# Attention layers of a hybrid encoder: the logits of two heads one behind the other

## The chip, the cores and the metric

The kernel runs on one core of one Trainium2 chip. Its time is the device time of one launch in microseconds (us). Before the change the median of 3 runs is 1270.73 us, from 1269.79 to 1271.33.

## The reference

Four layers over a sequence of 256 tokens of width 1024, all in float32. Layer 0 and layer 3 mix tokens with differential attention, layer 1 with a gated linear recurrence, layer 2 with a gated short convolution; every layer also has a 4-head cross-attention into 256 memory tokens, an output projection, a layer norm, a gated feed-forward part with a convolution of width 3, and a second layer norm. The attention, which the change concerns, is (cut):

```python
# differential attention, 6 heads, each with two maps of 64 columns
q = q.reshape(b, s, DA_HEADS, 2, DA_HD) * (DA_HD ** -0.5)
k = k.reshape(b, s, DA_HEADS, 2, DA_HD)
logits = jnp.einsum('bqhmd,bkhmd->bmhqk', qb, k).astype(jnp.float32) + bias
probs = jax.nn.softmax(logits, axis=-1)
w = (probs[:, 0] - lam * probs[:, 1]).astype(v.dtype)
o = jnp.einsum('bhqk,bkhe->bqhe', w, v)
o = _rms_norm(o, subln) * (1.0 - lam_init)
# cross-attention into the memory, 4 heads of 64 columns
probs = jax.nn.softmax(jnp.einsum('bshd,bmhd->bhsm', q, km), axis=-1)
recalled = jnp.einsum('bhsm,bmhd->bshd', probs, vm)
y = jnp.concatenate([mixed, recalled], axis=-1) @ w_o[layer]
```

## The kernel before

All weights stream from memory once, in chunks of two units of 128x1024 numbers. Each unit goes through three steps: its load into a ring of 5 raw buffers, a rounding to fp32r on ScalarE (`w_hi`, item "hi"), and the residual of that rounding on VectorE (`w_lo`, item "lo"). A matmul with weights is then three passes: high by high, high by low, low by high. A unit is rounded as soon as the half that used its buffer five units ago is done, so it is ready about four halves ahead of its use.

`make_schedule` (from L72) writes one list of items by hand. Every engine walks through the same list and does its own part of each item, in that order, so an item that waits on an engine holds all later items of that engine. A chunk contributes in this order: "hi" and "lo" of unit 2c+4, the first half of its matmuls, the items of the row with an even number, "hi" and "lo" of unit 2c+5, the second half (behind which ScalarE copies the result out of its bank: `post`), the items of the row with an odd number. In an attention layer the chunks behind XQ are QK0 to QK5 (queries and keys of one head), V0 to V2 (values of two heads) and the four chunks WO of the output projection. Chunk number n in this order has the rows 2n and 2n+1: row 13 stands behind V0, row 14 between the halves of V1, row 15 behind V1, row 16 between the halves of V2. In layer 0 two chunks for the memory come in ahead, and the rows are moved by 4.

The items of the attention are:

- "xlog" and "log" (TensorE L814, L825): the logits of two memory heads or of the two maps of one head, four matmuls of 64 rows by 256 columns in float32, which take two passes each. They fill two of the four banks ACC; item number n takes the banks 0 and 1 when n is even, 2 and 3 when it is odd, and waits until logits n-2 have been read. VectorE takes the row maxima (L1335; for "log" together with adding the bias, L1342, into `lg`).
- "xexp" and "exp" (ScalarE L1071): four exponentials with their sums. "xprob" and "prob" (VectorE L1359 to L1374): the probabilities.
- "xturn" and "turnw" (TensorE L837, L846): the transposes of the probabilities, into the side banks, with copies by ScalarE (L1081, L1086).
- "xpv" (L857) and "pv" (L870): probabilities by values. Behind the second head of a pair ScalarE copies the pair's output (L1092) and squares it (L1095).
- "ms" (VectorE L1384), then a power on GpSimd (L1453), and "tok" (VectorE L1390): the RMS norm of a pair. "scale" (TensorE L895, ScalarE L1101, VectorE L1400): its transposes, and the split of the result into `mixT_hi` and `mixT_lo`, the input of the output projection. Transposes of "scale" and of "turnw" use the same side bank, so a "turnw" behind a "scale" waits for that split.
- "seed" (ScalarE L1055): the output projection adds into the four banks ACC, which are first filled with the scaled residual stream, two banks per item. A seed waits until the last logits in its banks have been read, and WO's first matmul waits for all four.

`post` of QK number u waits for the logits of head u-2, because the two buffers of `qk` alternate. The two buffers of `prob` alternate too: a "prob" waits for the transposes of two items before.

Of the kernel before, what the change touches and what calls it, by code (L numbers as in the profile page):

```python
# [60 lines left out]
def layer_kind(layer):  # L61
    return ("attn", "hgrn", "conv")[layer % 3]


def make_schedule():
# [12 lines left out]
    def split_units(u):  # L78
        items.extend([("lo", u)] if u in rounded else [("hi", u), ("lo", u)])
# [32 lines left out]
    for layer in range(DEPTH):  # L112
        kind = layer_kind(layer)
        it = lambda name, *a: (name, layer, *a)
        chunk("F", "XQ", layer, 0)
        if layer == 0:
            items.extend([("bias_rows",), ("turn", "mem", 0)])
        if kind == "attn":
            order = [("F", "QK", h) for h in range(HEADS)] + [("T", "V", p) for p in range(PAIRS)]


            at = {0: [it("xlog", 0)], 1: [it("xexp", 0)], 2: [it("xprob", 0), it("xlog", 1)],
                  3: [it("xexp", 1), it("log", 0)], 4: [it("exp", 0), it("xprob", 1)],
                  5: [it("xturn", 0), it("log", 1)], 6: [it("exp", 1), it("prob", 0)],
                  7: [it("xpv", 0), it("log", 2)], 8: [it("xturn", 1), it("exp", 2), it("prob", 1)],
                  9: [it("xpv", 1), it("turnw", 0), it("log", 3)], 10: [it("exp", 3), it("prob", 2)],
                  11: [it("turnw", 1), it("log", 4)], 12: [it("exp", 4), it("prob", 3)], 13: [it("turnw", 2), it("log", 5)],
                  14: [it("exp", 5), it("prob", 4), it("pv", 0), it("pv", 1)],
                  15: [it("turnw", 3), it("ms", 0), it("tok", 0)], 16: [it("prob", 5), it("scale", 0)],
                  17: [it("turnw", 4), it("pv", 2), it("pv", 3)], 18: [it("turnw", 5), it("ms", 1), it("tok", 1)],  # L130
                  19: [it("scale", 1), it("pv", 4), it("pv", 5)], 20: [it("ms", 2), it("tok", 2)], 22: [it("scale", 2)]}
            at[13].append(("seed", 2 * layer, 0))
            at[15].append(("seed", 2 * layer, 1))
            if layer == 0:

                order[1:1] = [("F", "KM", 0), ("T", "VM", 0)]
                at = {h + 4: row for h, row in at.items()}
                at[0] = [("turn", "mem", 1)]
                at[5].append(("prepare",))
        elif kind == "conv":  # L140
            order = [("F", "CG", 0), ("F", "CG", 1), ("F", "CB", 0), ("F", "CG", 2), ("F", "CG", 3), ("F", "CB", 1),
                     ("F", "CG", 4), ("F", "CG", 5), ("F", "CB", 2)]
            at = {0: [it("xlog", 0), it("xexp", 0), it("xlog", 1), it("xexp", 1)], 1: [it("xprob", 0), it("xprob", 1)],
                  4: [it("xturn", 0)], 5: [it("xpv", 0)], 8: [it("xturn", 1)], 9: [it("xpv", 1)]}
            at.setdefault(9, []).extend([("seed", 2 * layer, 0), ("seed", 2 * layer, 1)])
        else:
            order = []
            for p in range(PAIRS):
                order += [("F", "FF", p), ("F", "FB", p), ("F", "HQ", p)]
            order += [("T", "HV", p) for p in range(PAIRS)]  # L150
            order += [("F", "HG", p) for p in range(PAIRS)]
            at = {0: [it("xlog", 0), it("xexp", 0), it("xlog", 1), it("xexp", 1)], 1: [it("xprob", 0), it("xprob", 1)],
                  4: [it("xturn", 0)], 5: [it("xpv", 0)], 6: [it("xturn", 1)], 7: [it("xpv", 1)]}
            at[26], at[28] = [("seed", 2 * layer, 0)], [("seed", 2 * layer, 1)]

            for p, first in enumerate((7, 14, 21)):
                for n in range(LEVELS + 1):
                    at.setdefault(first + n, []).append(it("level", p, n))
                    if n + 1 < LEVELS:
                        at[first + n].append(it("keys", p, n + 1))  # L160

            for p in range(PAIRS):
                c = len(chunks) + 3 * p
                at.setdefault(6 * p + 2, []).append(("gates", c))
                at.setdefault(6 * p + 4, []).append(("gates", c + 1))
                at.setdefault(6 * p + 5, []).append(it("sums", p))
                at.setdefault(6 * p + 6, []).extend([("q0", c + 2), it("queries", p, 0)])
                at.setdefault(6 * p + 7, []).insert(len(at[6 * p + 7]) if p else 0, it("queries", p, 1))
                at.setdefault(2 * (4 * PAIRS + p) + 2, []).append(("outgate", len(chunks) + 4 * PAIRS + p))
            for h, more in {20: [it("hpv", 0)], 22: [it("ms", 0)], 23: [it("tok", 0)], 24: [it("hpv", 1)],  # L170
                            25: [it("ms", 1)], 26: [it("scale", 0), it("tok", 1)], 29: [it("scale", 1)], 30: [it("hpv", 2)],
                            31: [it("ms", 2)], 32: [it("tok", 2)], 33: [it("scale", 2)]}.items():
                at.setdefault(h, []).extend(more)

        order += [("O", "WO", (n, pair)) for n, pair in enumerate((3, 0, 1))]
        for n, (form, role, index) in enumerate(order):
            chunk(form, role, layer, index, between=at.get(2 * n, []), after=at.get(2 * n + 1, []),
                  held=role == "WO" and index[0] == 2)

        def close(form, role, index, following):  # L180

            nonlocal norms
            c, m = len(chunks), norms
            chunks.append((form, role, layer, index))
            last = m == 2 * DEPTH - 1
            items.extend([("half", c, 0), ("stats", m, 0), ("hi", 2 * c - 1 + AHEAD), ("half", c, 1)])
            items.extend([("norm", m, 0), ("lo", 2 * c - 1 + AHEAD), ("hi", 2 * c + AHEAD)])
            items.append(("stats", m, 1))

            items.extend([("norm", m, 1), ("turn", m, 0)] if following else [("norm", m, 1)] if last else  # L190
                         [("turn", m, 0), ("norm", m, 1)])
            if following:
                items.append(("lo", 2 * c + AHEAD))
                chunks.append(following)
                items.extend([("half", c + 1, 0), ("part", c + 1)])
            elif not last:

                items.append(("warm",))
                items.append(("early", c + 1))
            items.append(("hi", 2 * c + 1 + AHEAD))  # L200
            if not last:
                items.append(("turn", m, 1))
            if following:
                items.append(("half", c + 1, 1))
            else:
                items.append(("lo", 2 * c + AHEAD))
            items.append(("lo", 2 * c + 1 + AHEAD))
            if following:
                split_units(2 * c + 2 + AHEAD)
                split_units(2 * c + 3 + AHEAD)  # L210
            norms += 1

        more = layer + 1 < DEPTH
        close("O", "WO", (3, 2), ("F", "KM", layer + 1, 0) if more else None)

        for g in range(GROUPS):
            chunk("F", "UA", layer, g)
            chunk("F", "UB", layer, g, after=[("seed", 2 * layer + 1, t) for t in range(TT)] if g == 0 else ())
            if 1 <= g <= GROUPS - 3:
                chunk("O", "DN", layer, (g - 1, g - 1))  # L220
        for g in (GROUPS - 3, GROUPS - 2):
            chunk("O", "DN", layer, (g, g), held=g == GROUPS - 2)
        close("O", "DN", (GROUPS - 1, GROUPS - 1), ("T", "VM", layer + 1, 0) if more else None)
# [4 lines left out]
def trunk_kernel(nc, stream, x, mem, rel_bias, ln, lam, subln, lower, hnorm, cconv, fconv,  # L228
                 ident_c, onehot_c, masks_c, out):
    chunks, items = make_schedule()  # L230
    nchunks = len(chunks)
    n_last_o = {layer: None for layer in range(DEPTH)}
# [1300 lines left out]
```

## Time and profile before

| what | value |
|---|---|
| median of 3 runs | 1270.73 us (1269.79 to 1271.33) |
| the profiled execution, its own time | 1269.29 us |
| its span, from the first to the last instruction | 1267.5 us |
| TensorE busy | 1252.7 us |
| VectorE busy | 1016.2 us |
| ScalarE busy | 728.8 us |
| mean granted clock of TensorE | 0.999 of full speed |

The profile comes from one execution. Its views name an engine as PE (TensorE), PEld (its weight loads, which overlap PE), DVE (VectorE), ACT (ScalarE), POOL (GpSimd); L12 is line 12 of the kernel. The chain of waits follows the work that ended last back from step to step; in it a matmul stands with the time that it adds, since matmuls overlap in a pipeline. In the timeline a row gives the start, the time from the first start to the last end of a run of like instructions, and the idle time in front. The end of a matmul is modelled, so distances between starts are what counts on TensorE. Layer 0's attention lies at about 33 to 125 us, layer 3's at about 973 to 1064 us.

### The profile page before, as it was taken

Reading aid. Unit: us, or ns where it says so; the run is one execution under the profiler, and the core shown is the slowest. Engines: PE = TensorE matmul, PEld = TensorE weight load, DVE = VectorE, ACT = ScalarE, POOL = GpSimd, SP = SyncE. Lnnn points to the kernel's source line nnn. Section 1 sums busy time; section 2 is a strip of 40 time slices with the busy share of each in tenths; the row PEclk is TensorE's granted clock in tenths of the full one; section 3 lists DMA queues with packets and bytes.
Section 4 is the critical chain, followed back from the end, with each engine's and each line's share of the span. In section 5 each row is a group of like instructions: output and inputs, shape, how many; then the busy total and the mean of one; then the engine's idle time right before and its main releaser. Section 6 shows DMA issues by size and latency. Waiting matters only on the chain.

```text
span 1267.5 us, 20453 instructions
## 1 busy us (share of the span) xinstructions
PE 1252.7 (99%) x7778; PEld 1108.1 (87%) x7778; DVE 1016.2 (80%) x1576; ACT 728.8 (58%) x1184; POOL 20.8 (2%) x29
## 2 busy tenths in 40 slices
PE   8999999999999999999999999999999999999997
PEld 6988888888999988888889998888889898888886
DVE  5775898888869888988888768988888776888887
ACT  5665665555676554655564635655564774655552
POOL 0000000000000010000000000000000000000000
PEclk9999999999999999999999999999999999999999
DMA  8734465665544345655555664665655443565561
GB/s 294 246 126 138 155 227 188 199 196 173 180 167 133 117 135 170 226 189 194 186 186 177 211 199 172 221 198 186 192 189 172 162 134 116 184 232 195 187 193 58
DMA packets 63389, 228.27 MB, mean 180 GB/s; under 512 B 7446, under 2 KB 9110, under 8 KB 62268
## 3 DMA queue, kind: packets, MB, share of 16 engines
q1 hardware_dynamic: 63292, 226.97, 54.3%
q8 instruction: 62, 1.02, 0.3%
q14 instruction: 35, 0.29, 0.1%
HBM read 225.88 MB, written 1.06 MB: 179 GB/s over the span
## 4 chain that ended last, share of the span: by engine, by line
PE 92%; DVE 5%; DMA 1%; issue 1%; ACT 1%; SPq 0%; DVEq 0%
PE pair L686 26%; PE acc L749 20%; PE pair L689 13%; PE pair L700 6%; PE pair L701 5%; PE pair L702 5%; PE pair L712 2%; PE pair L714 2%; PE pair L716 2%; PE pair L914 2%; PE acc L728 1%; PE acc L730 1%; PE acc L729 1%; DMA raw<-in_stream 1%; DVE w_lo L1132 1%; PE acc L825 1%
## 5 line engine op out<-in xcount | busy, mean ns | idle before, releaser
L1132 DVE TENSOR_TENSOR w_lo<-raw,w_hi 128x1024 fp32r<-128x1024 f32 x404 | 487.7, 1222 | 114.4 <-ACT w_hi L932 113.7
L932 ACT ACTIVATE w_hi<-raw 128x1024 fp32r<-128x1024 f32 x404 | 424.4, 1057 | 222.7 <-PE pair L689 69.1
L686 PE MATMUL pair<-xT,w_hi 128*128 128x512 f32 x1392 | 437.1, 395 | 1.0 <-DVE xT L1296 1.0
L689 PEld LDWEIGHTS pair<-xT,w_lo 128*128 128x128 f32 x1392 | 261.5, 188 | 61.5
L689 PE MATMUL pair<-xT,w_lo 128*128 128x256 f32 x1392 | 273.5, 278 | 0.0
L686 PEld LDWEIGHTS pair<-xT,w_hi 128*128 128x128 f32 x1392 | 214.3, 189 | 4.0 <-issue 1.5
L700 PE MATMUL pair<-xT,w_hi 128*128 128x256 f32 x592 | 171.3, 289 | 0.6 <-DVE xT L1296 0.6
L701 PE MATMUL pair<-xT,w_hi 128*128 128x256 f32 x592 | 167.4, 283 | 0.0
L702 PE MATMUL pair<-xT,w_lo 128*128 128x256 f32 x592 | 167.3, 283 | 0.0
L963 ACT ACTIVATE hid<-pair 128x512 f32<-128x512 f32 x88 | 52.4, 596 | 129.4 <-PE pair L689 128.6
L700 PEld LDWEIGHTS pair<-xT,w_hi 128*128 128x128 f32 x592 | 113.3, 191 | 6.9 <-issue 5.1
L701 PEld LDWEIGHTS pair<-xT,w_hi 128*128 128x128 f32 x592 | 113.5, 192 | 0.0
L702 PEld LDWEIGHTS pair<-xT,w_lo 128*128 128x128 f32 x592 | 113.4, 192 | 0.0
L1164 DVE TENSOR_TENSOR hid<-pair,hid 128x512 f32<-128x512 f32 x88 | 60.7, 690 | 50.9 <-ACT hid L963 50.9
L749 PE MATMUL acc<-w_hi,gT_hi 128*128 128x512 f32 x304 | 93.9, 390 | 0.0
L749 PE MATMUL acc<-w_lo,gT_hi 128*128 128x512 f32 x304 | 93.6, 389 | 0.0
L749 PE MATMUL acc<-w_hi,gT_lo 128*128 128x512 f32 x304 | 93.6, 389 | 0.0
L1009 ACT ACTIVATE cv<-hid,fconv_w 128x256 f32<-128x256 f32 x176 | 79.3, 499 | 16.0 <-DVE hid L1164 15.6
L1149 DVE SCALAR_TENSOR_TENSOR cv<-hid,fconv_w,cv 128x255 f32<-128x255 f32 x176 | 77.4, 481 | 3.1
L1145 DVE SCALAR_TENSOR_TENSOR cv<-hid,fconv_w,cv 128x255 f32<-128x255 f32 x176 | 76.9, 479 | 0.0
L749 PEld LDWEIGHTS acc<-w_lo,gT_hi 128*128 128x128 f32 x304 | 57.1, 188 | 12.2
L749 PEld LDWEIGHTS acc<-w_hi,gT_lo 128*128 128x128 f32 x304 | 57.1, 188 | 11.9
(185 smaller groups left out, 1605.5 us busy)
## 6 DMA issues: line engine op xcount, KB each, us to landing
raw<-in_stream SPq DMA_DIRECT2D x404, 512.0 KB, 4.5
gains<-in_ln SPq DMA_DIRECT2D x8, 1024.0 KB, 8.7
bias<-bias_scratch SPq DMA_DIRECT2D x2, 1152.0 KB, 8.8
x_tok<-in_x SPq DMA_DIRECT2D x2, 512.0 KB, 5.2
y_tok<-in_mem SPq DMA_DIRECT2D x1, 1024.0 KB, 11.7
out<-x_tok SPq DMA_DIRECT2D x4, 256.0 KB, 2.0
masks_in<-in_masks_c SPq DMA_DIRECT2D x1, 512.0 KB, 7.8
fconv_w<-in_fconv SPq DMA_DIRECT2D x1, 264.0 KB, 7.6
```

The source lines that it names most:

```text
L686: pe.matmul(bank, w_hi[:, slot, kk * P:(kk + 1) * P], xT[:, kk].rearrange("p a s -> p (a s)"), start=(kk == 0), stop=(kk == KT - 1), skip_ ...
L689: last = pe.matmul(bank[:, 0:SEQ], w_lo[:, slot, kk * P:(kk + 1) * P], xT[:, kk, 0, :], start=False, stop=(kk == KT - 1), skip_group_check ...
L700: pe.matmul(bank, w_hi[:, slot, at], a_hi(k, every), start=(k == 0), stop=False)
L701: pe.matmul(bank, w_hi[:, slot, at], a_lo(k, every), start=False, stop=False)
L702: last = pe.matmul(bank, w_lo[:, slot, at], a_hi(k, every), start=False, stop=(k == KT - 1))
L749: last = pe.matmul(ACC[2 * t + h][:], b(i, tok), w[:, slot, h * 512:h * 512 + 512], start=False, stop=False, skip_group_check=True)
L932: nc.scalar.activation(w_hi[:, u % SPLIT, :], raw[:, u % RAW, :], ACT.Copy).then_inc(hi_ready, 1)
L1009: last = nc.scalar.activation(cv[:, w, i, :], hid[:, w, i, :], ACT.Copy, scale=fconv_w[:, layer, 1, first + i:first + i + 1])
L1132: v.tensor_tensor(w_lo[:, u % SPLIT, :], raw[:, u % RAW, :], w_hi[:, u % SPLIT, :].bitcast(F32), ALU.subtract).then_inc(lo_ready, 1)
L1145: last = v.scalar_tensor_tensor(dst[i][:, 1:SEQ], src[i][:, 0:SEQ - 1], weights(0, i), dst[i][:, 1:SEQ], ALU.mult, ALU.add)
L1149: last = v.scalar_tensor_tensor(dst[i][:, 0:SEQ - 1], src[i][:, 1:SEQ], weights(2, i), dst[i][:, 0:SEQ - 1], ALU.mult, ALU.add)
L1164: v.tensor_tensor(hid[:, w], PAIR[proj_ord[c] % 2][:, :, 0:SEQ], hid[:, w], ALU.add).then_inc(hid_ready, 1)
```

## The change

The schedule of the attention layers is rewritten; no instruction is added or removed. The two "xlog" stand in one row, and the six "log" in three rows as pairs, (0, 1), (2, 3) and (4, 5), one behind the other, so that they take all four banks. "xturn" (0) comes behind the first pair, "xpv" (0) and (1) and "xturn" (1) get rows of their own, exps and probs move by one to three rows, and the seeds of the sums stand one row later each, at the end of their rows.

```diff
-            at = {0: [it("xlog", 0)], 1: [it("xexp", 0)], 2: [it("xprob", 0), it("xlog", 1)],
-                  3: [it("xexp", 1), it("log", 0)], 4: [it("exp", 0), it("xprob", 1)],
-                  5: [it("xturn", 0), it("log", 1)], 6: [it("exp", 1), it("prob", 0)],
-                  7: [it("xpv", 0), it("log", 2)], 8: [it("xturn", 1), it("exp", 2), it("prob", 1)],
-                  9: [it("xpv", 1), it("turnw", 0), it("log", 3)], 10: [it("exp", 3), it("prob", 2)],
-                  11: [it("turnw", 1), it("log", 4)], 12: [it("exp", 4), it("prob", 3)], 13: [it("turnw", 2), it("log", 5)],
-                  14: [it("exp", 5), it("prob", 4), it("pv", 0), it("pv", 1)],
-                  15: [it("turnw", 3), it("ms", 0), it("tok", 0)], 16: [it("prob", 5), it("scale", 0)],
+            at = {0: [it("xlog", 0), it("xlog", 1)], 1: [it("xexp", 0)], 2: [it("xexp", 1), it("xprob", 0)],
+                  3: [it("xprob", 1)], 5: [it("log", 0), it("log", 1), it("xturn", 0)],
+                  6: [it("exp", 0), it("xpv", 0)], 7: [it("exp", 1), it("prob", 0), it("xturn", 1)],
+                  8: [it("prob", 1), it("xpv", 1)], 9: [it("turnw", 0), it("log", 2), it("log", 3)],
+                  10: [it("exp", 2)], 11: [it("turnw", 1), it("exp", 3), it("prob", 2)],
+                  12: [it("prob", 3)], 13: [it("turnw", 2), it("log", 4), it("log", 5)],
+                  14: [it("exp", 4), it("pv", 0), it("pv", 1)],
+                  15: [it("turnw", 3), it("exp", 5), it("prob", 4), it("ms", 0), it("tok", 0)], 16: [it("prob", 5), it("scale", 0)],
                   17: [it("turnw", 4), it("pv", 2), it("pv", 3)], 18: [it("turnw", 5), it("ms", 1), it("tok", 1)],
                   19: [it("scale", 1), it("pv", 4), it("pv", 5)], 20: [it("ms", 2), it("tok", 2)], 22: [it("scale", 2)]}
-            at[13].append(("seed", 2 * layer, 0))
-            at[15].append(("seed", 2 * layer, 1))
+            at[14].append(("seed", 2 * layer, 0))
+            at[16].append(("seed", 2 * layer, 1))
```

## Rows read from the trace of the kernel before

**Rows 1.** The page, part 1: busy us, share of the span and instructions.
```profile
PE 1252.7 (99%) x7778; PEld 1108.1 (87%) x7778; DVE 1016.2 (80%) x1576; ACT 728.8 (58%) x1184; POOL 20.8 (2%) x29
```
**Rows 2.** Waits of TensorE over the whole span: total us, times, longest.
```profile
PE pair L846 <- DVE mixT_lo L1400: 0.7, 2, 0.3
```
**Rows 3.** Chain of waits, start us and us: logits in layers 3 and 1.
```profile
976.71 1.07 PE acc L814 x8
977.78 0.32 PE pair L700
...
340.01 2.03 PE acc L814 x16
```
**Rows 4.** Chain of waits, layer 3: xturn, xpv, turnw behind xpv, turnw alone.
```profile
994.89 0.87 PE pair L837 x8
...
1002.79 1.02 PE pair L857 x8
...
1012.71 0.59 PE pair L846 x4
...
1020.32 0.44 PE pair L846 x4
```
**Rows 5.** Timeline of TensorE, layer 3: start us, us, instruction, idle before it.
```profile
1032.20 1.95 PE L870 MATMUL pair<-v_tok,probT 128*128 128x128 f32 x16
...
1040.17 0.60 PE L895 MATMUL pair<-ident,a_out 128*128 128x128 f32 x4
...
1043.36 0.28 PE L716 MATMUL pair<-w_hi,xT 128*128 128x256 f32 x1
1043.98 0.63 PE L846 MATMUL pair<-ident,prob 128*128 128x128 f32 x4 [0.34 <-DVE mixT_lo L1400]
```
**Rows 6.** Timeline of ScalarE, layer 3: outputs' copy, rounding, seed 1, rounding.
```profile
1034.18 0.60 ACT L1092 ACTIVATE a_out<-pair 128x512 f32<-128x512 f32 x1 [1.06 <-PE pair L870]
...
1035.67 1.08 ACT L932 ACTIVATE w_hi<-raw 128x1024 fp32r<-128x1024 f32 x1
...
1038.03 1.12 ACT L1055 ACTIVATE acc<-x_tok 128x512 f32<-128x512 f32 x2
1039.07 1.06 ACT L932 ACTIVATE w_hi<-raw 128x1024 fp32r<-128x1024 f32 x1
```
**Rows 7.** Timeline of VectorE, layer 3: residual, ms, tok, prob's first instruction, split.
```profile
1036.79 1.22 DVE L1132 TENSOR_TENSOR w_lo<-raw,w_hi 128x1024 fp32r<-128x1024 f32 x1 [2.85 <-ACT w_hi L932]
1037.93 0.16 DVE L1384 TENSOR_SCALAR ms_eps<-ms_sum 128x4 f32<-128x4 f32 x1
1039.22 0.69 DVE L1390 TENSOR_TENSOR a_out<-a_out,ms_r 128x512 f32<-128x512 f32 x1 [1.13 <-POOL ms_r L1453]
...
1041.30 0.17 DVE L1365 RECIPROCAL row_inv<-row_sum 128x4 f32<-128x4 f32 x1
...
1043.09 0.74 DVE L1400 SCALAR_TENSOR_TENSOR mixT_lo<-pair,sub_gain,mixT_hi 128x512 fp32r<-128x512 f32 x1
```
**Rows 8.** Timeline of ScalarE, layer 3: post, rounding, transposed copies, first exp, rounding.
```profile
1002.82 0.38 ACT L953 ACTIVATE qk<-pair 128x256 f32<-128x256 f32 x1 [1.13 <-PE pair L702]
...
1003.37 1.06 ACT L932 ACTIVATE w_hi<-raw 128x1024 fp32r<-128x1024 f32 x1
1008.42 1.09 ACT L1081 ACTIVATE xprobT<-pair 128x512 f32<-128x512 f32 x2 [4.00 <-PE pair L837]
1009.39 0.51 ACT L1071 ACTIVATE ex<-lg,neg_max 128x256 f32<-128x256 f32 x1
...
1011.37 1.05 ACT L932 ACTIVATE w_hi<-raw 128x1024 fp32r<-128x1024 f32 x1
```
**Rows 9.** Timeline of TensorE, layer 3: xturn(1) and, one half later, xpv(1).
```profile
1007.79 1.04 PE L837 MATMUL pair<-ident,prob 128*128 128x128 f32 x8
...
1011.62 1.09 PE L857 MATMUL pair<-xprobT,vm 128*64 128x256 f32 x8
```
**Rows 10.** Stretch 18 to 22 us: length, busy us of each engine, granted clock, DMA.
```profile
18.00:22.00 4.00, 2.33 (x15) 1.29 (x14) 1.23 (x1) 2.12 (x4) 0.00 (x0) 1.00 0.67 262
```

## The prediction

> **What bounds the kernel now.** First the engines' shares of the span: TensorE is busy 1252.7 of 1267.5 us, VectorE 1016.2, ScalarE 728.8 [rows 1]. So a us that TensorE no longer spends is a us of the span, and work of the other engines counts only where TensorE comes to a wait and finds it unfinished. Then TensorE's waits over the whole run: the one in the attention layers that the change touches is the memory transposes of head 4 (L846) waiting for the split of the first normed pair (L1400), 2 times, 0.7 us in all, once in layer 0 and once in layer 3 [rows 2]. Both layers show the same instants 939.2 us apart, so I work in layer 3 and double.
>
> **What the joins are worth.** In the chain of waits a weight matmul takes 0.12 us after another weight matmul. The logits of one head (8 passes) take 1.07, and the weight matmul behind them 0.32, 0.20 more than usual: 1.27 for logits that stand alone [rows 3]. Layer 1 already puts two logits one behind the other: 2.03 for 16 passes [rows 3], with the same 0.20 behind them 2.23; two alone cost 2.54. The other small groups: transposes of a memory pair (xturn) 0.87 with nothing behind them, even in front of logits; memory values (xpv) 1.02, with 0.20 behind when a weight matmul follows; transposes of a head (turnw) 0.44 alone and 0.59 behind xpv [rows 4].
> Before, in program order: xlog0 1.27, xlog1 1.27, log0 1.27, xturn0+log1 0.87+1.07+0.20 = 2.14, xpv0+log2 1.02+1.07+0.20 = 2.29, xturn1 0.87, xpv1+turnw0+log3 1.02+0.59+1.07+0.20 = 2.88, turnw1+log4 0.44+1.07+0.20 = 1.71, turnw2+log5 1.71. Sum 15.41.
> After: the xlog pair 2.23; log0+log1+xturn0, where no row shows transposes behind logits: 2.03 + 0.87, and 0.15 as turnw costs more behind xpv (0.59 against 0.44; bounds 0 and the 0.20 of a weight matmul), 3.05; xpv0 1.22; xturn1 0.87; xpv1 1.22; turnw0+pair 0.44+2.03+0.20 = 2.67; turnw1 0.44; turnw2+pair 2.67. Sum 14.37. That is 1.04 us less in each attention layer (0.99 to 1.19 by the bounds). Three pairs of one kind come together, and xpv loses its neighbour twice, which is why it isn't four times 0.31. Two heads of the mixer in a pair read different buffers than layer 1's pair; if that cost the join all its gain, the term would be 0.
>
> **What the moves cost: the first normed pair.** This is the large term. From the start of pv(0), pv(1) on TensorE (1032.20) to the transposes of the normed pair (scale 0, 1040.17) TensorE has 7.97 us of work of its own [rows 5]: both pv, V1's second half, turnw3, V2's first half. Beside it runs the chain that scale 0 waits for: the copy of the heads' outputs starts 1.98 after pv's start, copy and squares take 1.49, then ScalarE rounds a weight unit, and VectorE's residual of that unit starts 1.12 after the rounding [rows 6, 7]; the residual holds 1.14, ms starts, tok 1.29 later, and tok holds 0.69 and is seen 0.15 after its end (as L846 starts 0.15 after L1400's end, 1043.98 against 1043.83) [rows 5, 7]. Sum 1.98+1.49+1.12+1.14+1.29+0.69+0.15 = 7.86. The slack is 0.11 us.
> The change puts two things in that chain. Seed 0 moves from row 13 to the end of row 14, behind pv(1)'s copy on ScalarE and ahead of the rounding: two copies, 1.04 us until the rounding starts [rows 6]. And prob(4) moves from row 14, where it ran while VectorE had nothing to do, to row 15 ahead of ms(0): the reciprocal to the next instruction is 1.79 [rows 7]. VectorE takes its instructions in order, so ms(0), the power on GpSimd, tok(0) and scale 0 wait for prob(4). exp(4) is no hindrance: counted from turnw2's start, VectorE has log(4)'s maxima at about 4.0 (log(4) is done at 1.6, and prob(3) with a residual holds VectorE to 2.4, then 1.6 for the maxima), four exps of 1.98 end at 6.0, and the copy behind them can't start before 0.52 + 2.03 + 2.98 + 1.98 = 7.5. New chain 7.86+1.04+1.79 = 10.69, TensorE's own work unchanged at 7.97: scale 0 waits 2.72 us, and V2's second half and all behind it with it. Bounds: 0.93 if prob(4) were hidden, 1.68 if the seed were, and 3.2 with one more ScalarE copy of 0.5 in the chain, above the value taken.
>
> **The other waits.** At turnw4 TensorE now waits: the last weight matmul starts at 1043.36, the transposes could follow at 1043.48 and start at 1043.98, 0.50 [rows 5]. After, counted from scale 0's start, TensorE needs 0.35+2.96 = 3.31 (the 3.31 from 1040.17 to 1043.48); VectorE is done with tok 0.23 before scale 0, and takes residual 1.14, prob(5) 1.79, then the split, which turnw4 sees 0.89 after its start: 3.59. Wait 0.28, so 0.22 is won back. exp(5) (row 15) stands behind the copies of V1 and turnw3 and ends about 14.0 us after turnw2's start; prob(5) begins at 16.2 - 0.23 + 1.14 = 17.1: hidden by the wait above. Seed 1 (row 16, 1.04) is over some 3 us before WO's first matmul needs the four sums.
> Early in the layer one transfer gets short. xturn(1)'s copies stand on ScalarE behind exp(1): from the end of QK3's second half 0.19 to see it, 0.55 for post's two copies, four exps 1.98, two transposed copies 1.09, 0.15 to be seen, 3.96 [rows 8]; TensorE goes from xturn to xpv over one half, as here from 1007.79 to 1011.62, in 3.83 [rows 9]. 0.12 us of wait at xpv(1), bounds 0 and 0.4. ScalarE's copy of QK2 now waits for log(0), one group longer; TensorE needs that bank only a chunk later. VectorE takes two heads' maxima in a row (2 times 1.6); w_lo is made four halves (some 12 us) ahead, which covers them, and what is left of the cover is over 8 us. The loads of raw follow the residuals; none moves by more than 3.5 us against the 15 of its ring.
>
> **Sum.** Per layer -1.04 + 2.72 - 0.22 + 0.12 = +1.58; two layers +3.16. The profiled execution took 1269.29 (span 1267.5) and would take 1272.45; against the median 1270.73, which is 1.44 above it, 1273.9.
>
> **A rule against the reading of the joins.** In rows 3 the 16 passes of two heads follow at the pitch of 8, with no overlap, though the halves of a head use different 64 partitions. The Trainium skill, TensorEngine Tiling (Array Packing), Key Properties, says that different tiles can load and multiply in parallel. By that rule the second half of one head could run beside the first half of the next: up to 4 passes of 0.12 in each of the four pairs, 1.9 us per layer more; the trace of layer 1's pair speaks against it.
>
> **Rivals.**
> (a) The wait at scale 0 doesn't come, as the normed pair turns out not to be what its transposes wait for in this order, and only the joins are left: with xpv(1)'s 0.12, 1270.73 - 2 x 0.92 = 1268.9, not slower. For it: TensorE shows no wait there now. Against: the chain's slack is 0.11 and ScalarE and VectorE keep their order. The change is faster as long as less than 0.92 of the 2.72 arrives. 12 in 100.
> (b) The seed is hidden, as ScalarE has room ahead of the rounding elsewhere; prob(4) alone counts: 3.16 - 2.08 = +1.08, 1271.8. Against it: the seed waits behind the copy in program order. 11 in 100.
> (c) The pairs of the mixer's heads gain nothing (other buffers): +2.08 on top, 1276.0. 8 in 100.
> (d) TensorE's clock falls to 1.2 GHz in the new wait of 2.72 us. Around the longest wait of today, 1.67 us between 18 and 22 us, the granted clock stays at 1.00, 2.4 GHz [rows 10]. If V2's second half then ran at double its 2.96: +5.9, 1279.8. 4 in 100. The Trainium skill, TensorE: Matmul & The Clock Gate, section Why this matters for your kernels, warns that idle gaps between bursts of matmuls bring the clock down; no row here shows such a fall.
> (e) Tiles of two heads run side by side, by the rule above: -3.8 on top, 1270.1. 3 in 100.
>
> **Chances and range.** The forecast has 62 in 100, with its own range 1272.7 to 1275.3 (joins and waits each off by some tenths, medians by half a us). A comparison of this kernel tells about 0.2% (2.5 us) from no change. Slower by more: 0.52 of the forecast's 0.62, (c) and (d): 0.64. Within: the rest of the forecast, (b), (e), most of (a): 0.30. Faster: the lower edge of (a): 0.06. The range goes from just below (a)'s value to just short of (c)'s: 1268.5 to 1275.5.
>
> **What would show it.** A new TensorE wait at L895 for a_out of L1390, 2 times, some 2.7 us each; VectorE's order residual, prob, ms, tok with no idle time between the first three; the L814 and L825 passes at 2.03 us for 16; 0.3 us left of the wait at L846; a short wait at L857. Wrong it is if L895 starts on time, if the pairs take 2.14 for 16 passes, or if TensorE waits for w_lo.

## The result, and the profile after

| kernel | median us | lowest to highest | ratio to before, 95% interval |
|---|---|---|---|
| before | 1270.78 | 1269.79 to 1271.33 | |
| changed | 1275.18 | 1272.98 to 1276.9 | 1.0035 [1.0024, 1.0045] |

The change makes the kernel 4.4 us slower; 1273.9 was forecast. The profiled execution of the changed kernel took 1276.9 us (span 1275.1), 7.6 more than the profiled one of before, so its trace has to be read with care: it holds more than the medians differ by.

First the engines' busy time and TensorE's waits over the whole span (us in total, times, longest), in answer to [rows 1] and [rows 2]. Lines of the changed kernel stand one number higher than before, L896 for L895 and so on.

```profile
PE 1255.5 (98%) x7778; PEld 1114.3 (87%) x7778; DVE 1015.0 (80%) x1576; ACT 727.6 (57%) x1184; POOL 20.8 (2%) x29
```
```profile
PE pair L896 <- DVE a_out L1391: 4.9, 2, 2.5
```

A new wait heads the list: the transposes of the first normed pair wait for the normed pair, once per attention layer. L847's wait for L1401 is gone from it. The timeline of TensorE in layer 3 (start us, us, instruction, idle before it) answers to [rows 5]:

```profile
1036.11 1.95 PE L871 MATMUL pair<-v_tok,probT 128*128 128x128 f32 x16
...
1043.96 0.28 PE L717 MATMUL pair<-w_hi,xT 128*128 128x256 f32 x1
1046.71 0.97 PE L896 MATMUL pair<-ident,a_out 128*128 128x128 f32 x4 [2.47 <-DVE a_out L1391]
1047.33 0.56 PE L713 MATMUL pair<-w_hi,xT 128*128 128x256 f32 x1
1047.69 0.41 PE L715 MATMUL pair<-w_lo,xT 128*128 128x256 f32 x1
1047.90 0.41 PE L717 MATMUL pair<-w_hi,xT 128*128 128x256 f32 x1
...
1051.60 0.60 PE L847 MATMUL pair<-ident,prob 128*128 128x128 f32 x4
```

From pv to the transposes it is now 10.60 us, where it was 7.97. And behind the wait something else is to be seen: weight matmuls start 0.21 us apart (1047.69, 1047.90) instead of 0.12. The clock says why (stretch, its length, busy us of PE, PEld, DVE, ACT and POOL with instructions, granted clock, DMA share, GB/s):

```profile
1042.50:1046.50 4.00, 1.74 (x15) 1.53 (x13) 2.81 (x9) 3.07 (x10) 1.01 (x1) 1.00 0.42 131
1046.50:1048.50 2.00, 1.79 (x9) 1.79 (x10) 1.97 (x6) 0.79 (x2) 0.00 (x0) 0.60 0.00 0
1048.50:1050.30 1.80, 1.80 (x11) 1.80 (x10) 1.70 (x4) 1.80 (x3) 0.00 (x0) 0.50 0.72 189
1050.30:1052.30 2.00, 2.00 (x19) 2.00 (x19) 1.23 (x1) 0.59 (x3) 0.00 (x0) 1.00 0.24 92
```

TensorE had been busy without a wait until 2.47 us before; at the wait's end its granted clock goes to the lower level, 1.2 GHz, and stays there for some 3.5 us. Between the two transposes, 1046.71 and 1051.60, lie 4.89 us, against 3.31 of work at full speed and 3.81 before, where 0.50 of it was a wait.

The chain that set the time of the transposes, on VectorE, answers to [rows 7]:

```profile
1041.74 1.23 DVE L1133 TENSOR_TENSOR w_lo<-raw,w_hi 128x1024 fp32r<-128x1024 f32 x1 [4.66 <-ACT w_hi L933]
1042.89 0.17 DVE L1366 RECIPROCAL row_inv<-row_sum 128x4 f32<-128x4 f32 x1
...
1044.67 0.16 DVE L1385 TENSOR_SCALAR ms_eps<-ms_sum 128x4 f32<-128x4 f32 x1
1045.96 0.69 DVE L1391 TENSOR_TENSOR a_out<-a_out,ms_r 128x512 f32<-128x512 f32 x1 [1.12 <-POOL ms_r L1454]
```

and on ScalarE, to [rows 6]:

```profile
1038.09 0.60 ACT L1093 ACTIVATE a_out<-pair 128x512 f32<-128x512 f32 x1 [1.60 <-PE pair L871]
...
1039.59 1.15 ACT L1056 ACTIVATE acc<-x_tok 128x512 f32<-128x512 f32 x2
1040.63 1.08 ACT L933 ACTIVATE w_hi<-raw 128x1024 fp32r<-128x1024 f32 x1
```

Copy and squares from 1038.09, then the seed to 1040.63, the rounding, the residual at 1041.74 (VectorE idle for 4.66 us in front of it), prob(4) to 1044.67, and only then ms. (The description above has exps and probs move by one to three rows. In the diff the exps move by one or two, prob(0), (2) and (4) by one, and prob(1), (3) and (5) keep their rows.)

The joins are there too, in the chain of waits (start us, us), with the order of logits and transposes that no row of before had, in answer to [rows 3] and [rows 4]:

```profile
981.58 2.03 PE acc L815 x16
983.61 0.32 PE pair L701
...
998.20 2.03 PE acc L826 x16
1000.23 1.03 PE pair L838 x8
...
1011.96 1.09 PE pair L858 x8
```

**Where 7.6 us of the two profiled executions went.** From the pair of xlog to WO's long run of matmuls behind pv(5) in layer 3 (before 976.71 to 1054.66, after 981.58 to 1062.25) the changed kernel took 80.67 us against 77.95: +2.72. It divides at three instants that both traces show. Up to pv(0) (1032.20 and 1036.11) the changed kernel is 0.96 us shorter: that is what the joins gave, the short wait at xpv(1) taken off. From pv(0) to the pair's transposes it is 2.63 longer, from there to turnw4 (the transposes of head 4, L847) 1.08 longer, and behind them 0.03 shorter. The same stretch of layer 0 has +2.75. The other 2.1 us lie ahead of the first logits of layer 0, where nothing was changed: the first load took 7.95 us instead of 7.42, and the clock was low from about 22.9 to 26.3 us, behind a wait of 1.72 us; the kernel before has that wait as well, 1.67 us, and no fall behind it:

```profile
22.00:24.00 2.00, 2.00 (x15) 2.00 (x14) 0.91 (x2) 1.54 (x3) 0.00 (x0) 0.73 0.43 122
24.00:26.30 2.30, 2.30 (x12) 2.30 (x12) 1.60 (x2) 0.49 (x1) 0.00 (x0) 0.50 0.69 207
```

That fall at the launch is no part of the change. Of the profiled executions of the kernels below, those of seed_out, fill_wait, scale_first, old_prob_late and old_scale_first have it too; those of prob_back, both_out and old_seeds_late don't, and nor does that of before.

### The profile page after: what moved, and what is told of

The parts are those of the page before. It is cut to its first block, busy times and chain, and to the rows that moved or that the text cites. A ratio compares the mean times of both kernels' runs of the same rounds, so it can differ in the third digit from the quotient of the medians.

```text
span 1275.1 us, 20453 instructions
## 1 busy us (share of the span) xinstructions
PE 1255.5 (98%) x7778; PEld 1114.3 (87%) x7778; DVE 1015.0 (80%) x1576; ACT 727.6 (57%) x1184; POOL 20.8 (2%) x29
## 3 DMA queue, kind: packets, MB, share of 16 engines
q8 instruction: 62, 1.02, 0.3%
## 4 chain that ended last, share of the span: by engine, by line
PE 92%; DVE 5%; DMA 1%; issue 1%; ACT 1%; POOL 0%; SPq 0%; DVEq 0%; ACTq 0%
PE pair L687 25%; PE acc L750 20%; PE pair L690 13%; PE pair L701 6%; PE pair L702 5%; PE pair L703 5%; PE pair L713 2%; PE pair L715 2%; PE pair L717 2%; PE pair L915 2%; PE acc L729 1%; PE acc L731 1%; PE acc L730 1%; DMA raw<-in_stream 1%; DVE w_lo L1133 1%; PE acc L826 1%
```

## The experiments

Eight kernels, each compared with runs of the kernel before on the same chip (its medians there 1270.83 and 1270.56). "Distance" is from the start of pv(0) to the start of the first normed pair's transposes in layer 3; its own work there takes TensorE 7.97 us. "Stretch" is from the start of the xlog pair (or the first xlog) to WO's long run in layer 3, against the 77.95 us of before; it leaves the launch out.

| kernel | median us | ratio, 95% interval | distance us | idle at the pair's transposes, at turnw4 (longest) | stretch us |
|---|---|---|---|---|---|
| changed | 1275.18 | 1.0035 [1.0024, 1.0045] | 10.60 | 2.5, none | 80.67, +2.72 |
| prob_back | 1270.96 | 1.0006 [0.9997, 1.0014] | 8.82 | 0.7, 1.0 | 78.55, +0.60 |
| seed_out | 1271.96 | 1.0011 [1.0002, 1.0020] | 9.56 | 1.4, 0.7 | 78.98, +1.03 |
| both_out | 1276.34 | 1.0038 [1.0024, 1.0052] | 7.97 | none, 2.3 | 80.59, +2.64 |
| fill_wait | 1273.65 | 1.0024 [1.0014, 1.0034] | 10.60 | filled, 0.2 | 79.49, +1.54 |
| scale_first | 1266.90 | 0.9976 [0.9967, 0.9985] | 7.97 | none, none | 76.47, -1.48 |
| old_prob_late | 1274.16 | 1.0030 [1.0018, 1.0042] | 9.55 | 1.4, 0.2 | 79.39, +1.44 |
| old_seeds_late | 1272.37 | 1.0014 [1.0005, 1.0022] | 8.82 | 0.7, 0.2 | 78.65, +0.70 |
| old_scale_first | 1270.08 | 0.9992 [0.9983, 1.0001] | 7.98 | none, none | 77.42, -0.53 |

Small differences of medians have to be read beside the stretch, as the fall of the clock at the launch is worth about 1.5 us and comes unequally often. Profiled executions without any fall have a mean granted clock of 0.999, those with the launch's alone 0.997 or 0.998, that of both_out with two falls in the attention 0.996, the changed kernel's with all three 0.995. Of the two sets of before, 5 of 25 and 12 of 27 executions have 0.999 or more, of prob_back 7 of 11, of scale_first 6 of 10, of old_scale_first none of 11. Why they differ so isn't known, and that an execution without a trace can be sorted in this way is inferred, not shown.

**prob_back**: the changed kernel, prob(4) where it was.

```diff
-14: [it("exp", 4), it("pv", 0), it("pv", 1)],
-15: [it("turnw", 3), it("exp", 5), it("prob", 4), it("ms", 0), it("tok", 0)],
+14: [it("exp", 4), it("prob", 4), it("pv", 0), it("pv", 1)],
+15: [it("turnw", 3), it("exp", 5), it("ms", 0), it("tok", 0)],
```

> The changed kernel with prob(4) back in row 14, behind exp(4); seed 0 stays at row 14's end. Theory (the chain in front of the first normed pair's transposes grew by seed 0, 1.04 us, and prob(4), 1.79 us, over a slack of 0.11): the wait at L896 shrinks from 2.7 us from start to start to 0.9, per layer -1.04 + 0.93 - 0.22 + 0.12 = -0.2, so 1270.4 us, and TensorE's clock, which fell behind the wait of 2.5 us, stays at full speed. Rival (the wait comes from exp(5) or from the pairs of logits, and prob(4)'s place is of no account): the wait stays at 2.5 us and the time near 1275.

The distance fell from 10.60 to 8.82, by prob(4)'s 1.79, and the time by 4.2 us to about that of the kernel before, some of it the clock, which stayed up. The wait at the pair's transposes came out as forecast. What did not is the wait at turnw4: from start to start it is 1.20 us (4.51 - 3.31; 0.99 idle) instead of the 0.28 taken; more of it below. So the median, 0.6 us from the forecast, flatters it: the stretch is +0.60 per layer where -0.2 was worked out. The median seems to hide this because more executions of prob_back than of before have no fall at the launch (those at 0.999: median 1270.77 against 1269.51, +1.3 us, about twice 0.60).

**seed_out**: the changed kernel, seed 0 one row later.

```diff
-at[14].append(("seed", 2 * layer, 0))
+at[15].append(("seed", 2 * layer, 0))
```

> The changed kernel with seed 0 moved on to the end of row 15, behind the rounding that VectorE waits for; prob(4) stays ahead of ms(0). Theory: 1.04 us go from the chain, the wait at L896 is 1.7 us from start to start, per layer -1.04 + 1.68 - 0.22 + 0.12 = +0.54, so 1271.9 us, if the clock stays up after a wait of 1.5 us idle (before, 1.67 us idle left it at full speed); 1 to 2.5 us more where it falls. Rival (the seed is hidden): the wait stays at 2.5 us, 1275 us.

Distance 9.56, by the seed's 1.04 less than 10.60, and 1271.96 us. The rival (b) of the prediction, a hidden seed, has fallen. The clock in the half behind the wait of 1.44 us stayed up, and the time fell by 3.2 us, more than the 2.1 us of the seed in two layers. Here too turnw4 waits longer than forecast (0.67 us idle, 0.88 from start to start), and the stretch is +1.03 instead of +0.54; two layers of that would give 1272.9, so that the median is 1271.96, as forecast, has some luck in it.

**both_out**: both edits.

> The changed kernel with both edits: prob(4) back in row 14 and seed 0 at the end of row 15. Theory: the chain has its old 7.86 us against 7.97, no wait at L896; only the joins are left, per layer -1.04 - 0.2 + 0.12, together -2.3 us: 1268.5 us, faster than before. Rival (the pairs of logits themselves cost something elsewhere): 1270.8 or more with no wait at L896.

This forecast failed, by 8 us and in sign. The wait at the pair's transposes is gone as expected, but turnw4 waits 2.31 us, and the clock falls behind that wait. First TensorE's timeline of this kernel, then VectorE's and ScalarE's, then the granted clock:

```profile
1045.56 0.28 PE L717 MATMUL pair<-w_hi,xT 128*128 128x256 f32 x1
1048.15 0.91 PE L847 MATMUL pair<-ident,prob 128*128 128x128 f32 x4 [2.31 <-DVE mixT_lo L1401]
```
```profile
1041.42 0.69 DVE L1391 TENSOR_TENSOR a_out<-a_out,ms_r 128x512 f32<-128x512 f32 x1 [1.12 <-POOL ms_r L1454]
1044.33 1.23 DVE L1133 TENSOR_TENSOR w_lo<-raw,w_hi 128x1024 fp32r<-128x1024 f32 x1 [2.21 <-ACT w_hi L933]
1045.47 0.17 DVE L1366 RECIPROCAL row_inv<-row_sum 128x4 f32<-128x4 f32 x1
...
1047.26 0.74 DVE L1401 SCALAR_TENSOR_TENSOR mixT_lo<-pair,sub_gain,mixT_hi 128x512 fp32r<-128x512 f32 x1
```
```profile
1041.71 0.50 ACT L1072 ACTIVATE ex<-lg,neg_max 128x256 f32<-128x256 f32 x1
...
1042.20 1.11 ACT L1056 ACTIVATE acc<-x_tok 128x512 f32<-128x512 f32 x2
1043.24 1.05 ACT L933 ACTIVATE w_hi<-raw 128x1024 fp32r<-128x1024 f32 x1
```
```profile
1048.10:1050.10 2.00, 1.95 (x10) 1.98 (x11) 1.03 (x1) 0.60 (x1) 0.00 (x0) 0.56 0.18 74
```

The split of the normed pair (L1401), which turnw4 waits for, stands behind prob(5) and a residual, and that residual (idle 2.21) waits for a rounding which ScalarE does only after exp(5) and the seed. The prediction had written exp(5) off as "hidden by the wait above". It was hidden as long as that wait was there. With it gone, three things stand in front of the split: exp(5) in its new place, row 15 for row 14 (1.97 us, 1040.23 to 1042.20), the seed that this run itself put behind it (1.04), and prob(5) (1.79). How much is exp(5)'s is shown in part only. old_seeds_late below has the same order as prob_back from pv(0) on except that exp(5) is in row 14: there the residual starts without idle time and turnw4 comes 3.67 us behind the pair's transposes, in prob_back the residual is 0.74 idle for the rounding behind exp(5) and turnw4 comes 4.51 behind. No run moves exp(5) alone in the changed kernel, and scale_first below leaves it in row 15 and has no wait, with the seed and prob(5) out of the way.

**fill_wait**: the changed kernel, TensorE busy through most of the wait.

```diff
+FILL = 10
 ... (cut)
+                    if p == 0 and layer_kind(layer) == "attn":
+                        n = proj_ord[last_half]
+                        pe.wait_ge(*proj_read(n - 1))
+                        for _ in range(FILL):
+                            pe.matmul(PROJ[(n - 1) % 2], mixT_hi[:, 6, 0:P], mixT_hi[:, 6:8, :].rearrange("p a s -> p (a s)"),
+                                      start=True, stop=True)
                     pe.wait_ge(tok_ready, ordinal[pos] + 1)
```

> The changed kernel as it is, with 10 matmuls of 512 columns (2.2 us, their result is not used) on TensorE in front of the transposes of the first normed pair in both attention layers, in a bank that nobody uses then. They fill the wait and leave the chain alone. Theory (the wait costs 2.7 us, and the fall of the clock behind it another 1.2 to 1.3 us per layer in the executions where it falls): transposes start at the same distance from the pv matmuls, 10.7 us, the granted clock stays at 1.00 behind them, and the time is 1273.5 to 1274, with less scatter than the 1273.0 to 1276.9 of the changed kernel. Rival (the clock's fall is a matter of the launch and not of the wait): the stretch behind the transposes still runs at 0.5 of full speed, 1275 us.

This separates the wait from the clock. The transposes start at the same distance, 10.60. TensorE's timeline and the granted clock behind them in layer 3:

```profile
1042.96 2.46 PE L897 MATMUL pair<-mixT_hi 128*128 128x512 f32 x10
1045.59 0.66 PE L903 MATMUL pair<-ident,a_out 128*128 128x128 f32 x4 [0.18 <-DVE a_out L1398]
1049.27 0.63 PE L848 MATMUL pair<-ident,prob 128*128 128x128 f32 x4 [0.15 <-DVE mixT_lo L1408]
```
```profile
1046.50:1048.50 2.00, 2.00 (x19) 2.00 (x19) 1.93 (x8) 2.00 (x4) 0.00 (x0) 1.00 0.34 86
```

The clock is at 2.4 GHz, and turnw4 follows 3.68 us behind the transposes, against 4.89 in the changed kernel: the fall costs 1.21 us per layer where it comes. (The low clock stretches 3.31 us of work by 1.58, but with the clock up 0.37 of that would be a wait at turnw4.) In layer 0 it is the same: 3.68 against 4.90. The time is 1273.65, within 1272.4 to 1274.6, and the stretch is +1.54 per layer; the prediction, for waits and joins alone, had 1273.9 and +1.58. The rival of this run has fallen: its profiled execution has the fall at the launch and none in the attention layers, so the one behind the wait comes from the wait. The medians say the same more weakly, as the intervals of the two ratios, [1.0014, 1.0034] and [1.0024, 1.0045], overlap.

**old_prob_late** and **old_seeds_late**: one part of the change each, made alone on the kernel before.

```diff
-14: [it("exp", 5), it("prob", 4), it("pv", 0), it("pv", 1)],
-15: [it("turnw", 3), it("ms", 0), it("tok", 0)],
+14: [it("exp", 5), it("pv", 0), it("pv", 1)],
+15: [it("turnw", 3), it("prob", 4), it("ms", 0), it("tok", 0)],
```

> The kernel before with one part of the change: prob(4) from row 14 to row 15, ahead of ms(0). Theory: the chain grows from 7.86 to 9.65 us against TensorE's 7.97: L896 waits 1.7 us from start to start, L847 0.3 instead of 0.5, per layer +1.46, 1273.7 us. Rival (the old order's idle time on VectorE covers it): no wait at L896, 1270.8 us.

```diff
-at[13].append(("seed", 2 * layer, 0))
-at[15].append(("seed", 2 * layer, 1))
+at[14].append(("seed", 2 * layer, 0))
+at[16].append(("seed", 2 * layer, 1))
```

> The kernel before with the other part: seed 0 from row 13 to the end of row 14, seed 1 from row 15 to the end of row 16. Theory: the chain is 8.90 us against 7.97, L896 waits 0.9 us from start to start, L847 0.3, per layer +0.71, 1272.2 us. Rival (ScalarE has room): 1270.8 us.

Both came out within 0.5 us, and in the stretch within 0.02: +1.44 and +0.70 for +1.46 and +0.71. With the old logits in place, each move alone makes the wait: distances 9.55 and 8.82 for 9.65 and 8.90 forecast. So neither needs the pairs of logits.

**old_scale_first**: the kernel before, prob(5) behind scale 0.

```diff
-16: [it("prob", 5), it("scale", 0)],
+16: [it("scale", 0), it("prob", 5)],
```

> The kernel before with prob(5) behind scale 0 in row 16 and nothing else. Theory: the split follows the residual directly, so L847 no longer waits its 0.5 us, 2 times: 1269.8 us. Rival (prob(5) is then late for turnw5, or the split is held by ScalarE's copy): the wait moves and the time is 1270.8 us or more.

L846's wait is gone, and the next "turnw" isn't late. In time the interval holds both no change and the 1 us forecast, so the medians don't decide. The stretch of the one trace has the 0.5 us: 77.42 against 77.95. In every execution of this kernel the clock (0.997 or 0.998) looks as if it had fallen at the launch.

**scale_first**: the changed kernel's pairs with the four items in a better order.

```diff
-14: [it("exp", 4), it("pv", 0), it("pv", 1)],
-15: [it("turnw", 3), it("exp", 5), it("prob", 4), it("ms", 0), it("tok", 0)], 16: [it("prob", 5), it("scale", 0)],
-at[14].append(("seed", 2 * layer, 0))
+14: [it("exp", 4), it("prob", 4), it("pv", 0), it("pv", 1)],
+15: [it("turnw", 3), it("exp", 5), it("ms", 0), it("tok", 0)], 16: [it("scale", 0), it("prob", 5)],
+at[16].append(("seed", 2 * layer, 0))
```

> The changed kernel with prob(4) back in row 14, prob(5) behind scale 0 in row 16, and seed 0 behind both in row 16, ahead of seed 1. Theory (behind the first wait stands a second chain, exp(5) at its new place, a rounding, a residual, prob(5) and only then the split that turnw4 waits for; it is that chain that held the kernel with both edits): neither L896 nor L847 waits, all that is left are the joins and the 0.5 us that L847 waits before the change, per layer -1.04 - 0.50 + 0.1, so 1267.9 us, faster than before. Rival (the pairs of logits cost something that no wait shows): not under 1270.

It beats both kernels: 0.9976 [0.9967, 0.9985], 3.7 us below before. Of that about 3.0 are the schedule's (twice the 1.48 below; executions at 0.999 alone: 1266.59 against 1269.47), the rest fits fewer falls at the launch. TensorE has no wait at either place:

```profile
1031.29 1.95 PE L871 MATMUL pair<-v_tok,probT 128*128 128x128 f32 x16
...
1039.26 0.60 PE L896 MATMUL pair<-ident,a_out 128*128 128x128 f32 x4
1042.57 0.60 PE L847 MATMUL pair<-ident,prob 128*128 128x128 f32 x4
```

The stretch from the xlog pair to WO's long run takes 76.47 us (976.76 to 1053.23) against 77.95 before: -1.48 per layer, where -1.44 was worked out. old_scale_first alone has -0.53, so some 0.95 us of it are the pairs'. They are worth having; it is what was moved around them that made the change slow.

## Why the prediction was right, point by point

- **The joins**: -1.04 us per layer forecast, and -0.92 with the wait at xpv(1); -0.96 measured, up to pv(0). Pairs take 2.03 us everywhere, the heads' pairs like layer 1's, and xturn behind logits 1.03 where 0.87 + 0.15 was taken. Rivals (c) and, with passes that never overlap, (e) are out. The Trainium skill's TensorEngine Tiling (Array Packing), Key Properties, lets different tiles multiply in parallel; in this trace of pairs they don't: 16 passes, issued four to a tile in turn, take 2.03 us, twice the 1.07 of 8 but for one entry.
- **The chain in front of the pair's transposes**: 10.69 us worked out, 10.60 measured, and its two parts taken out or put in alone four times, each within 0.1 us. This step is shown. The 0.1 us is one term: tok's end was taken to be seen after 0.15 us, and the transposes start 0.06 behind it (1046.71 against 1046.65). So the old chain is about 7.77, not 7.86, and its slack 0.2, not 0.11.
- **turnw4**: 0.28 us of wait forecast. In the changed kernel it has none, since the low clock stretches TensorE's work in front of it; with the clock up (fill_wait) it is 0.15 idle and 0.37 from start to start (3.68 - 3.31), so 0.13 won back where 0.22 was forecast.
- **xpv(1)**: 0.12 forecast; 1.09 instead of 1.02 in the chain, 0.07.
- **The clock**: the step that was under-priced. Rival (d) had 4 in 100 and a price of 5.9 us, as if all of V2's second half ran at the low clock; the fall did come, on top of the forecast and smaller: 1.21 us per layer in the profiled execution. The forecast of 1273.9 has no term for it, and its absence is most of what is missing to 1275.18: filling the wait brings 1273.65. Whether it falls in each execution of the changed kernel isn't known, as only one has a trace. The mean clocks suggest that it doesn't: two of the seven, at 0.998, took 1272.98 and 1273.31 us, the five at 0.996 or 0.995 1274.44 to 1276.9.
- The Trainium skill, TensorE: Matmul & The Clock Gate, section Why this matters for your kernels, warns of idle gaps between bursts. This trace agrees in kind and not in size: 2.47 and 2.31 us (both_out) idle stand ahead of a fall, 1.43 and 1.44 (old_prob_late, seed_out) don't, and all of these gaps are shorter than those that the section warns of, so here the measurement decides.
- [rows 10], at 1.67, were read as safe. The changed kernel's launch has a fall behind 1.72. Of the ten profiled executions six have one at that place, behind 1.66 to 1.88 us idle, and four have none, behind 1.67 to 1.84. So that row was one execution's luck, and the length of that wait alone doesn't say whether the clock falls. The same reading stands in the expectation of seed_out; its 1.44 us held.
- **Luck in the number**: the range ended at 1275.5 because of rival (c), not of the clock, and the median lies 0.3 us inside it; two of the seven executions, 1275.6 and 1276.9, lie outside. What the runs confirm is the mechanism and its size without the fall (+1.54 per layer for +1.58), not the edge of the range.
- **What was written off**: "exp(5) ... hidden by the wait above" was true and misleading. It has a part in the wrong forecasts of both_out and of turnw4 in prob_back and seed_out.
- The 1.44 us between the profiled execution of before and its median, taken over as a constant, fits the launch: that execution has no fall there, and the changed kernel's lost about 1.5 us by one (2.05 us later, less 0.53 for the load). Executions of before at 0.999 or more have medians of 1269.51 and 1269.47 in the two sets, those below it 1270.91 and 1271.28. This is an inference: only one execution of before has a trace.

## What to carry to other kernels

Where one engine is the bound and the others are told their order by hand, write for each of its waits the sum of the chain behind it and of its own work beside it, and keep the difference: here it was 0.1 to 0.2 us, and of 2.83 us of harmless-looking work, on engines busy 58% and 80%, 2.63 went straight into the time. An item that a wait hides isn't free: list it as the next chain, for whoever removes the wait. And price a new wait of TensorE with the clock behind it; a few matmuls whose result nobody reads can be cheaper than the silence. Where the effect is as small as the scatter, compare a stretch that lies between two instants of the traces, and not the medians alone: they hit the forecast of prob_back when its trace had missed it by 0.8 us per layer.

## What the runs showed of the hardware

- Behind 2.3 to 2.5 us without work in this stage TensorE's granted clock went to 1.2 GHz for about 3.5 us, in each of the four traced cases (both layers of the changed kernel and of both_out); behind 1.4 us it stayed at 2.4 GHz. At the launch it fell behind 1.7 to 1.9 us in six of ten profiled executions and not in the other four.
- Ten matmuls of 512 columns in the wait (2.46 us; 2.2 had been expected) kept it up and saved 1.21 us of the following 4.89.
- Float32 logits of 64 rows keep their pitch of 0.12 us per pass across two heads (1.07 us for 8 passes, 2.03 for 16); what a pair saves is one entry and one exit.
